# Openings of three units, a shorter norm chain, and a last product in two halves of tokens, in a two-block transformer kernel

## The reference

```python
def _rmsnorm(x, g):
    xf = x.astype(jnp.float32)
    return xf * lax.rsqrt(jnp.mean(xf * xf, axis=-1, keepdims=True) + NORM_EPS) * g.astype(jnp.float32)

# first block
h = _rmsnorm(x, norm_mix_pre)
y = mixers(h @ w_in)                                 # rwkv7, mlstm, windowed and forgetting attention
x = x + _rmsnorm(y @ w_out, norm_mix_post)
h = _rmsnorm(x, norm_ffn_pre)
gate, up = jnp.split(h @ ffn_w_up, 2, axis=-1)       # 2816 columns each
f = jax.nn.gelu(_causal_dwconv(gate, ...)) * up
x = x + _rmsnorm(f @ ffn_w_down, norm_ffn_post)

# second block
x = x + 0.5 * swiglu(rmsnorm(x, ffn1_norm), ffn1_w_gate, ffn1_w_up, ffn1_w_down)
x = x + hybrid_mixer(rmsnorm(x, mix_norm), w_in, ..., w_out)
x = x + 0.5 * swiglu(rmsnorm(x, ffn2_norm), ffn2_w_gate, ffn2_w_up, ffn2_w_down)
return rmsnorm(x, final_norm)
```

## Time and profile before

| | |
|---|---|
| median of 3 runs | 1740.0 us |
| profiled execution | 1741.66 us |
| its span in the profile | 1739.8 us |
| TensorE (PE) busy | 1654.2 us, 95% |
| VectorE (DVE) busy | 820.3 us, 47% |
| ScalarE (ACT) busy | 697.7 us, 40% |
| GpSimd (POOL) busy | 289.2 us, 17% |
| mean granted TensorE clock | 0.981 |
| HBM traffic | 84 GB/s over the span |

### The profile page before, as it was taken

How to read it: one execution, slowest core, us unless ns; L and a number is a source line. 1 busy time by engine, 2 the same in 40 slices (tenths; PEclk the granted TensorE clock), 3 DMA queues, 4 the chain that set the end, 5 groups by cost and what they waited for, 6 DMA issues and landing times.

```text
span 1739.8 us, 21730 instructions
## 1 busy us (share of the span) xinstructions
PE 1654.2 (95%) x8578; PEld 1338.9 (77%) x8578; DVE 820.3 (47%) x1276; ACT 697.7 (40%) x1255; POOL 289.2 (17%) x241
## 2 busy tenths in 40 slices
PE   6999998988999999979999999999999999999995
PEld 5776776667888888858888888878887788888884
DVE  4566344355655542255444433367455444444332
ACT  5556445545433333245333332244533433333222
POOL 1221110023222210022222210000010122222001
PEclk9999998989999999999999999999999999999998
DMA  4220011121332233313222323322132232232331
GB/s 166 85 74 26 14 49 37 58 100 61 110 97 97 97 93 98 100 49 109 97 97 97 97 88 101 103 80 86 37 101 83 72 112 96 99 97 93 98 100 58
DMA packets 44133, 148.37 MB, mean 85 GB/s; under 512 B 5064, under 2 KB 6144, under 8 KB 44032
## 3 DMA queue, kind: packets, MB, share of 16 engines
q1 hardware_dynamic: 40032, 140.53, 24.9%
q10 hardware_dynamic: 4000, 6.46, 1.1%
HBM read 144.86 MB, written 2.10 MB: 84 GB/s over the span
## 4 chain that ended last, share of the span: by engine, by line
PE 87%; DVE 6%; ACT 5%; issue 1%; POOL 1%; DMA 0%; DVEq 0%; ACTq 0%; POOLq 0%
PE bank L198 76%; PE bank L335 6%; PE bank L304 3%; DVE t L170 3%; ACT t L158 2%; DVE t L180 2%; ACT L158 1%; PE bank L206 1%; DVE t L261 1%; ACT t L257 1%; POOL t L170 1%; DVE t L184 0%; DMA t<-in_cst 0%; DVE t L190 0%; ACT t L165 0%
## 5 line engine op out<-in xcount | busy, mean ns | idle before, releaser
L198 PE MATMUL bank<-t 128*128 128x512 f32 (+6 forms) x7578 | 1516.3, 360 | 26.8 <-DVE t L170 10.0
L198 PEld LDWEIGHTS bank<-t 128*128 128x128 f32 (+3 forms) x7578 | 1161.1, 179 | 296.8 <-issue 36.8
L261 DVE TENSOR_TENSOR t<-t 128x512 fp32r<-128x512 f32 (+1 forms) x516 | 394.3, 795 | 436.4 <-ACT t L257 428.8
L170 POOL TENSOR_TENSOR t<-t 128x512 f32<-128x512 f32 (+1 forms) x181 | 239.4, 1322 | 1210.0 <-DVE t L170 563.3
L257 ACT ACTIVATE t<-t 128x512 fp32r<-128x512 f32 (+1 forms) x540 | 310.7, 613 | 261.2 <-PE bank L335 216.9
L158 ACT ACTIVATE t<-t 128x512 f32<-128x512 f32 (+6 forms) x351 | 202.6, 605 | 357.7 <-DVE t L170 169.6
L170 DVE TENSOR_TENSOR t<-bank,t 128x512 f32<-128x512 f32 (+4 forms) x238 | 147.4, 630 | 237.2 <-PE bank L335 213.7
L335 PE MATMUL bank<-t 128*128 128x512 f32 x516 | 200.7, 389 | 0.0
L165 ACT ACTIVATE t<-t 128x512 fp32r<-128x512 f32 (+3 forms) x87 | 51.7, 606 | 250.0 <-POOL t L170 247.6
L170 DVE TENSOR_TENSOR t<-t 128x512 f32<-128x512 f32 (+7 forms) x135 | 96.6, 733 | 72.2 <-ACT t L158 62.0
L180 DVE SCALAR_TENSOR_TENSOR t<-t 128x512 f32<-128x512 f32 (+3 forms) x142 | 104.0, 748 | 39.7 <-ACT t L158 38.3
(11 more groups left out here) (22 smaller groups left out, 90.0 us busy)
## 6 DMA issues: line engine op xcount, KB each, us to landing
t<-in_ffn_w_up SPq DMA_DIRECT2D x88, 512.0 KB, 4.4
t<-in_w_in SPq DMA_DIRECT2D x50, 512.0 KB, 3.5
t<-in_ffn_w_down SPq DMA_DIRECT2D x48, 512.0 KB, 3.5
t<-in_ffn_w_gate SPq DMA_DIRECT2D x44, 512.0 KB, 3.4
t<-in_ffn_w_down SPq DMA_DIRECT2D x24, 384.0 KB, 3.1
t<-in_w_out SPq DMA_DIRECT2D x16, 512.0 KB, 3.5
t<-in_xt SPq DMA_DIRECT2D x8, 256.0 KB, 5.9
t<-in_xt ACTq DMA_DIRECT2D x8, 256.0 KB, 4.6
```

The costliest lines, as they stand in the source:

```text
L170: return q.do(lambda e: e.tensor_tensor(out, a, b, op), *deps, us=self.cost(out, q, True))
L198: fn = lambda e: e.matmul(out, w, x, start=start, stop=stop, skip_group_check=True)
L261: q.put(lambda e: e.tensor_tensor(lo, raw, hi.bitcast(F), SUB), self.s_tail[i % 2], 1, (self.s_head, i + 1), before, us=0.79 if q is self. ...
```

## The change

- `open` takes the place of `pair` and of the third unit: it runs three units. First, over k, the hi·hi and lo·hi matmuls of all three, which need `head(k)` only; then, over k, the hi·lo matmuls, which need `tail(k)`. The six pieces of the three units stay in use until the second pass. There is a semaphore of used pieces for each buffer (`s_used[n]`).
- `square_in` has a flag `own` that puts the even sums on VectorE too; `pre_norm` and the last even result before a post norm use it.
- Post norm: the two sums of n < 7 are multiplied with ones during product 7 (`sums`), and the square of y[7] is added by a matmul of its own (`rest`). The Ln table is loaded ahead of the products (`log_table`). `add_post` does all additions on VectorE, and the tails after all heads.
- The end (`finale`): the last product runs as two halves of 256 tokens (`half`). Sums, Ln, Exp, scaling and stores of the first half are put under the second. Scaling by gain and `rB` is one VectorE instruction. There are 16 stores of 128 KB, 12 from SyncE's queue and 4 from ScalarE's.

```diff
     def split(self, i):
...
-                      (self.s_load[u % RAW], 16 * (u // RAW + 1)), (self.s_used, i - CUT + 1), us=0.62)
+                      (self.s_load[u % RAW], 16 * (u // RAW + 1)), self.used(i - CUT) if i >= CUT else None, us=0.62)
...
+    def open(self, outs, xh, heads, xl, *free):
+        pe, at = self.p.pe, self.at
+        part = lambda t, u, k: t[(at + 2 * u + k // 4) % CUT][:, (k % 4) * 128:(k % 4) * 128 + 128]
+        self.ahead(CUT)
+        for k in range(8):
+            for u, out in enumerate(outs):
+                i = at + 2 * u + k // 4
+                self.p.mm(out, part(self.hi, u, k), xh[k], k == 0, False, heads[k], (self.s_head, i + 1), *free)
+            for u, out in enumerate(outs):
+                self.p.mm(out, part(self.lo, u, k), xh[k], False, False, self.tail(at + 2 * u + k // 4))
+        for k in range(8):
+            for u, out in enumerate(outs):
+                fn = lambda e, o=out, w=part(self.hi, u, k), x=xl[k][0], z=k == 7: e.matmul(
+                    o, w, x, start=False, stop=z, skip_group_check=True)
+                if k % 4 == 3:
+                    pe.put(fn, self.used(at + 2 * u + k // 4)[0], 1, xl[k][1], us=0.227)
+                else:
+                    pe.quiet(fn, xl[k][1], us=0.227)
+        self.at += 2 * len(outs)
+        return [self.used(at + 2 * u + 1) for u in range(len(outs))]
...
     def product(self, W, banks, xh, xl):
         if self.rms:
-            two = [banks.next(), banks.next()]
-            m = W.pair([b.t[:, :] for b in two], xh, xl, *[b.free for b in two])
-            self.done = list(zip(two, m))
-            yield
-            self.third = W.parts(self.extra.t[:, :], 1, xh, xl, self.extra.free)
-            next(self.third)
+            three = [banks.next(), banks.next(), self.extra]
+            m = W.open([b.t[:, :] for b in three], xh, W.p.heads, xl, *[b.free for b in three])
+            self.done = list(zip(three, m))
             self.rms()
             self.rms = None
+            yield
...
                     if f == 0:
-                        mg, mu = W.pair([bg.t[:, :], bu.t[:, :]], xh, xl, bg.free, bu.free)
-                        early = W.product(bank[2].t[:, :], 1, xh, xl, bank[2].free)
+                        three = [bg, bu, bank[2]]
+                        mg, mu, early = W.open([b.t[:, :] for b in three], xh, p.heads, xl, *[b.free for b in three])
                         p.rms()
...
+        def rest(b, src, *deps):
+            a = p.act(sq[1][:, :], src, ACT.Square, state["sq"][1], *deps)
+            state["sq"][1] = m = p.mm(b.t[:, :], ones, sq[1][:, :], False, True, a, last=True)
+            W.ahead(CUT - 1)
+            b.free, state["rB"] = rstd_of(b.t[:, :], 1.0 / 1024, eps[:, 0:1], rB[:, :], m, state.get("rB_read"))
+            return a
...
+        def add_post(then, y, yt):
             for n in range(8):
                 a = p.tt(y[n][:, :], y[n][:, :], rB[:, :], MUL, yt[n], state["rB"])
-                xtok[n] = p.tt(xt[n][:, :], xt[n][:, :], y[n][:, :], ADD, a, xtok[n], q=p.dv if n % 4 == 0 else p.po)
-                heads.append(head(n, then))
-                if n:
-                    made[n - 1] = tail(n - 1, then, heads[n - 1])
-            made[7] = tail(7, then, heads[7])
+                xtok[n] = p.tt(xt[n][:, :], xt[n][:, :], y[n][:, :], ADD, a, xtok[n])
+                begun[n] = head(n, then)
+                if n == 1:
+                    W.ahead(CUT)
+            for n in range(8):
+                made[n] = tail(n, then, begun[n])
...
+        def finale(scale, xh, xl):
...
+            a0 = add(0, W.half(outs[0].t[:, cols[0]], xh, xl, cols[0], {}, outs[0].free))
+            got = {}
+            def first():
+                sums_of(0)
+                got["r"] = rstd(0, a0)
+                log_table()
+            m = W.half(outs[1].t[:, cols[1]], xh, xl, cols[1], {7: first, 12: lambda: sums_of(1)}, outs[1].free)
+            write(0, range(4), got["r"])
+            a1 = add(1, m)
+            write(0, range(4, 8), got["r"])
+            write(1, range(8), rstd(1, a1))
```

More of the change, by code:

```diff
@@ L1 @@
+import itertools
 import math
@@ L1636, in pre_norm @@
             for k in range(8):
-                if made[k] is None:
-                    made[k] = tail(k, gain, head(k, gain))
+                if begun[k] is None:
+                    begun[k] = head(k, gain)
+                    made[k] = tail(k, gain, begun[k])
             W.ahead(CUT)
@@ L1699, in ffn @@
                 yt = []
-                for n in range(8):
+                if post or not then:
+                    log_table()
+                for n in range(8 if then else 7):
                     b = bank[4 + n % 2]
-                    m = W.product(b.t[:, :], 3, [t[:, :] for t in fH],
-                                  [(fL[i][:, :], fl[i]) for i in range(22)], b.free)
-                    if post:
-                        square_in(n, b.t[:, :], m)
+                    g = W.parts(b.t[:, :], 3, [t[:, :] for t in fH],
+                                [(fL[i][:, :], fl[i]) for i in range(22)], b.free)
+                    m = ended(g, 3, (lambda: sums(bank[6])) if post and n == 7 else None)
+                    if post and n == 7:
+                        yt.append(add_last(y[n], post, b, m, bank[6]))
+                    elif post:
+                        square_in(n, b.t[:, :], m, own=n == 6)
                         b.free = t = p.act(y[n][:, :], b.t[:, :], ACT.Copy, m, scale=col(post, n))
@@ new lines, in ended, with add_last @@
+        def ended(g, n, then):
+            for i in itertools.count(1):
+                try:
+                    next(g)
+                except StopIteration as end:
+                    return end.value
+                if i == n and then:
+                    then()
+        def add_last(y, post, b, m, into):
+            a = rest(into, b.t[:, :], m)
+            b.free = t = p.ts(y[:, :], b.t[:, :], col(post, 7), None, MUL, None, a)
+            return t
+        def add_post(then, y, yt):
@@ L1743, in project_out @@
                         b = bank[n % 2]
-                        m = W.product(b.t[:, :], 1, xh, xl, b.free)
-                    if post:
-                        square_in(n, b.t[:, :], m)
+                        m = ended(W.parts(b.t[:, :], 1, xh, xl, b.free), 1,
+                                  (lambda: sums(bank[2])) if post and n == 7 else None)
+                    if post and n == 7:
+                        yt.append(add_last(y[n], post, b, m, bank[2]))
+                    elif post:
+                        square_in(n, b.t[:, :], m, own=n == 6)
                         b.free = t = p.act(y[n][:, :], b.t[:, :], ACT.Copy, m, scale=col(post, n))
@@ L1756, in project_out @@
                 if post:
-                    add_post(then, y, yt, bank[2])
+                    add_post(then, y, yt)
         def done_all():
```

123 lines of the change are left out of this document (76 added, 47 removed).

## The result

The changed kernel takes 1781.1 us (median of 4 runs, 1780.1 to 1785.6) where the kernel before takes 1740.6 (4 runs in the same sessions, 1739.8 to 1741.8): a ratio of 1.0237, with a 95% interval of 1.0218 to 1.0256. It is slower by 2.4%. The forecast was 1773 with a range of 1752 to 1787. The profiled execution of the changed kernel took 1780.1 us (span 1778.3); against the span of before, 1739.8, it is 38.5 longer, and the sum in the prediction had 33.2.

The account below looks back on a forecast made before the run. It took TensorE, busy 95% of the span, as the bound: its matmuls, pauses and end. Opening losses 31.9 plus clock 8.0 minus the end's 6.7 gave +33.2 us, so 1773 from the 1740.0 median, range 1752 to 1787.

Parts of the forecast that it names:

- The cover goes: After each opening's sums TensorE waits for a split queued behind the norm: 10.1, 10.1, 8.1, 5.5 and 8.1 us.
- Breaks in the openings: In mixer 1, mixer 2 and the last FFN, TensorE stops after five matmuls for the third unit's lo part.
- Mixers 20.0: Mixer 1 loses 9.8 us and mixer 2 7.0, plus 3.2 of clock after their waits.
- Last FFN 13.8: The last FFN's opening loses 12.2 us, plus 1.6 of clock after its wait.
- The two FFNs behind a post norm, 6.1: Convolved FFN loses 2.4 us and second FFN 0.5, plus 3.2 of clock after their waits.
- Both delays go: In the post norm, delays of 0.69 and 1.14 us before Ln vanish, so Exp ends 1.8 earlier.
- Clock after the new waits, 8.0: After each of five waits TensorE runs 3.4 us at half clock, 1.6 lost each, 8.0 us in all.
- The end −6.7: Half-width last product, with the first half's norm and stores under the second, shortens the end from 35.0 to 28.3 us.
- rival 2: At the end, half-width matmuls save nothing because each still loads 128 weight columns: 14.1 us more, 1787; chance 0.09.
- Rival 1: Mixers absorb their late openings, so the losses of 9.8, 7.0 and 3.2 us vanish: 1753; chance 0.11.
- Rival 3: Split pieces are ready after the sums in all five openings, so the kernel gets faster: 1723 us; chance 0.05.

Follow-up runs that it names:

- experiment 3: Changed kernel with four splits issued ahead of Ln in each opening and the fifth behind Exp: 1749.7 us, ratio 1.0054.
- experiment 5: Changed kernel with the old opening (pair, half of the third unit, norm) in mixer 1 and mixer 2 alone: 1759.1 us, ratio 1.0107.
- experiment 6: Changed kernel with the old opening (pair, third unit, norm) in the last FFN alone: 1764.2 us, ratio 1.0144.
- experiment 8: Changed kernel with old openings and old order of heads, tails and additions in the two FFNs behind a post norm, new norm chain kept: 1773.9 us.
- experiment 7: Changed kernel with the old end (last product at full width, final norm behind it): 1788.0 us, ratio 1.0282.
- the candidate: Changed kernel with three-unit openings only in the two FFNs behind a post norm, four splits before Ln, fifth behind Exp, old openings elsewhere: 1725.45 us.
- experiment 10: The candidate with one sum in place of two inside the last product before each post norm, VectorE adding the square sums first: 1724.4 us.

## Why the prediction came out right, point by point

The medians are 40.5 us apart where the sum had 33.2, inside the range. The mechanism it named is the one that the runs show; the sum is short in three terms.

- *The cover goes.* Right, in mechanism and size. The five waits were 43.5 us for 41.9. Moving the splits ahead of Ln shortened them to some 12 (experiment 3), and the time followed, by 31.4 us.
- *Breaks in the openings.* Half right. TensorE does stand for the third unit in mixer 1, mixer 2 and the last FFN, but it breaks off after one or two matmuls and not after five. I let the third unit's hi part be there and made it wait for the lo; the last FFN's rows are

```profile
1386.89 0.73 PE L199 MATMUL bank<-t 128*128 128x512 f32 x2 [2.06 <-ACT t L159]
1391.70 8.60 PE L199 MATMUL bank<-t 128*128 128x512 f32 x29 [4.08 <-ACT t L259]
```

  line 259, ScalarE's hi part. With three matmuls more to do than the sum had, under 1 us a stage, the restart came where the sum had it in the last FFN, and 0.8 to 1.5 us sooner in the two mixers, so hardly anything was lost by it.
- *Mixers 20.0* (9.8 + 7.0 + 3.2). Right: 22.0 by experiment 5.
- *Last FFN 13.8* (12.2 + 1.6). Short by 3: 16.9 by experiment 6. By the trace 0.6 is a longer wait and 0.9 clock (2.5 for 1.6). In the trace another 1.1 arises ahead of it, in the second block's output projection, where the half clock lasts longer than before; experiment 6 has that too, so it is no part of the 16.9, and the rest stays open.
- *The two FFNs behind a post norm, 6.1* (2.4 + 0.5 + 3.2). This is the term that was mis-sized: by the trace they lose 5.7 and 5.3, 11.0. The step that failed is "Both delays go (0.69+1.14): Exp [...] ends 1.8 earlier". They do go: from the end of the last product to the end of Exp it is 4.54 in experiment 8 and in the changed kernel, for 6.34; but I didn't price what paid for them, the sums placed inside the last product, 1.7 us on TensorE's path. TensorE's start, counted from where the same matmuls of the last product stood, came 1.9 earlier and not 3.7. So when the opening's sums begin TensorE is 5.6 and 5.3 us ahead of the kernel before, where the sum had a lead of 7.6: 4.3 of the 4.9 that is missing. The sums and the wait together are 0.8 and 0.9 longer than in the sum, and the half clock in the convolved FFN cost 2.4 for 1.6. Two things that the sum didn't have work against each other: the Ln table's load ahead of the output projection costs 1.2, and the later pause that went away gives 3.0 back. Without that luck the term would have been short by 8.
- *Clock after the new waits, 8.0.* Right: 9.6 by the idle matmuls, 11.2 by the lengths of the stretches, and the upper bound was 16. The Trainium skill (TensorE: Matmul & The Clock Gate, HAM oscillation in real kernels) says that an idle gap puts TensorE back to half rate. This case's trace agrees: the pauses of 5.3 to 10.6 us did, all five times, and no such stretch came where they were filled.
- *The end −6.7.* Right: −6.9 by experiment 7. A 256-column matmul took 0.12, so rival 2 (nothing saved by half width) is out. The Trainium skill (the same page, Back-to-back issue gap) gives 262 cycles, 0.109 us, for it; this trace shows more, 0.120.
- *Rival 1* looked half true in the trace, since mixer 1 gave 5 us back. Experiment 5 shows that it wasn't slack: see the last section. By the two traces the stages' terms and the end add up to 43.6, 10.4 more than the sum, and this luck took off 5.1 of it, so the total (38.5 for 33.2) is nearer than its terms deserve.
- *Rival 3* had the right condition to look at, but the wrong price. It put the kernel at 1723 if the pieces were there after the sums, and drew the line at 16.6 us of waits together. Experiment 3 has some 12 and takes 1749.7, where rival 3's own sum would give 1735. What it lacked is, by the traces, mainly the half clock behind the mixers' two waits for a bank (5.8), the smaller leads behind the post norms (4.3) and the table load (1.2). Where three units in a row do have their gain, behind the post norms, the candidate has it.

## What to carry to other kernels

When a block of matmuls is made to use every prefetch buffer, look at what the next block's prefetch is queued behind on the engine that makes it: here a few 0.6 us splits behind Ln and Exp cost TensorE 5 to 11 us each time, and issuing them a few lines earlier made a change that lost 2.4% into one that, kept to the stages with a cause for it, gains 0.8%. Issue no more of them early than have their data, or the engine blocks on the load with the urgent work behind it. A chain that is shortened by moving work elsewhere has to be charged with that work on the engine that sets the time.

## What the runs showed of the hardware that was not expected

**The clock inside an unchanged stage.** TensorE's instructions in mixer 1 from 206 us on are the same before and after the change, yet the same stretch of it (280 matmuls) took 49.7 us in the kernel before and 46.5 in the changed one. The candidate and the kernel of experiment 10 don't differ at all up to 360 us, and their traces have 46.5 and 49.8. The two windows of it, first of the candidate, then of the other:

```profile
215.10:218.40 3.30, 3.30 (x21) 2.69 (x22) 0.48 (x2) 1.32 (x4) 0.00 (x0) 1.00 0.00 0
242.40:245.70 3.30, 3.30 (x20) 2.82 (x20) 1.59 (x6) 0.00 (x0) 1.29 (x1) 1.00 0.25 60
```

```profile
215.10:218.40 3.30, 3.30 (x11) 2.93 (x12) 0.42 (x1) 0.96 (x4) 0.00 (x0) 0.50 0.00 0
242.40:245.70 3.30, 3.30 (x9) 2.64 (x9) 1.76 (x5) 0.80 (x2) 1.28 (x1) 0.50 0.00 0
```

The granted clock in them is 1.00 or 0.50 with the same instructions and start times within 0.8 us. Over a longer stretch, from 206 us to near mixer 1's end, it took 96.3, 94.8, 93.1 or 91.6 us in different kernels. So 5 us of "given back" in a comparison of two single traces can be this alone. What sets it was not found, nor whether it is settled anew in each execution: there is one trace for each kernel. In experiment 10 the traced execution was the slowest of the five, 1727.8 us with a mean granted clock of 0.984, and the others took 1721.3 to 1724.4 at 0.987 or 0.988, which speaks for it. An effect of that size needs the medians at least.

**A matmul of two fp32 operands** 512 columns wide is two records of 0.427 us, where one on the split pieces is one of 0.227: such an idle matmul in a pause takes 0.854, nearly four times as long.
